# Gated mixer of two linear layers: order of the inverse, the key-query products, the roots, silu and table loads

## What is computed

```python
def chunk_gated_delta_rule(q, k, v, g, beta):
    gc = jnp.cumsum(g, axis=-1)
    seg = jnp.exp(jnp.where(incl, gc[..., :, None] - gc[..., None, :], -jnp.inf))
    kb = k * beta[..., None]
    a_mat = jnp.where(strict, jnp.einsum("nbhid,nbhjd->nbhij", kb, k) * seg, 0.0) + jnp.eye(L, dtype=f32)
    rhs = jnp.concatenate([v * beta[..., None], kb * jnp.exp(gc)[..., None]], axis=-1)
    sol = lax.linalg.triangular_solve(a_mat, rhs, left_side=True, lower=True, unit_diagonal=True)
    u, w = sol[..., :HEAD_DIM], sol[..., HEAD_DIM:]
    qk = jnp.einsum("nbhid,nbhjd->nbhij", q, k) * seg
    q_dec = q * jnp.exp(gc)[..., None]
    k_dec = k * jnp.exp(gc[..., -1:] - gc)[..., None]
```

## Time and profile before

| | us |
|---|---|
| median of 3 runs | 3536.49 (3536.39 to 3537.64) |
| profiled execution, its own time | 3531.68 |
| its span, first to last instruction | 3529.8 |
| TensorE matmul busy | 3402.0 (96% of the span) |
| VectorE busy | 1994.3 (56%) |
| ScalarE busy | 1165.2 (33%) |
| GpSimd busy | 332.8 (9%) |
| mean granted TensorE clock | 0.985 |

### The profile page before, as it was taken

The page is one execution under the profiler, slowest core; times in us unless marked ns, Lnnn a source line. Parts: engine busy times, 40 slices in busy tenths (PEclk is TensorE's granted clock), DMA queues, the critical chain, the costliest instruction groups (busy, mean ns, idle before and its releaser), DMA issues.

```text
span 3529.8 us, 49652 instructions
## 1 busy us (share of the span) xinstructions
PE 3402.0 (96%) x18508; PEld 2802.1 (79%) x18508; DVE 1994.3 (56%) x3164; ACT 1165.2 (33%) x1766; POOL 332.8 (9%) x293
## 2 busy tenths in 40 slices
PE   7999999889999999999988999999999999999999
PEld 5888877678888888887767888886778888688887
DVE  6763457667642566354766764446666625766642
ACT  4222344433221322234443322133443314343321
POOL 0000100231000000010023100111200011120002
PEclk9999999989999999999998999999999999999999
DMA  7653222104533355322210454321222332122232
GB/s 294 219 190 102 91 88 80 36 15 148 190 132 107 132 190 191 102 92 82 84 37 15 148 190 136 106 84 60 72 84 95 108 101 67 58 74 98 98 104 82
DMA packets 100835, 386.77 MB, mean 110 GB/s; under 512 B 11134, under 2 KB 12286, under 8 KB 99800
## 3 DMA queue, kind: packets, MB, share of 16 engines
q1 hardware_dynamic: 100696, 384.82, 31.8%
HBM read 382.65 MB, written 2.12 MB: 109 GB/s over the span
## 4 chain that ended last, share of the span: by engine, by line
PE 86%; DVE 7%; ACT 3%; issue 1%; DMA 1%; POOL 0%; SPq 0%; ACTq 0%; DVEq 0%; POOLq 0%
PE bank L2889 18%; PE bank L2888 18%; PE bank L2890 18%; PE bank L3014 4%; PE bank L3016 4%; PE bank L3015 4%; PE bank L2899 1%; PE bank L2901 1%; PE bank L2900 1%; PE bank L2964 1%; PE bank L2963 1%; PE bank L2962 1%; PE bank L3102 1%; PE bank L3623 1%; PE bank L3625 1%
## 5 line engine op out<-in xcount | busy, mean ns | idle before, releaser
L1119 ACT ACTIVATE wH<-wR 128x1024 fp32r<-128x1024 f32 (+2 forms) x378 | 429.2, 1135 | 1399.6 <-PE bank L2890 1305.4
L1687 DVE TENSOR_TENSOR wL<-wR,wH 128x1024 fp32r<-128x1024 f32 (+2 forms) x384 | 509.5, 1327 | 595.0 <-ACT wH L1119 590.3
L2888 PE MATMUL bank<-hH,wH 128*128 128x512 f32 x1920 | 747.7, 389 | 4.1 <-DVE wL L1687 4.1
L2889 PE MATMUL bank<-hH,wL 128*128 128x512 f32 x1920 | 747.6, 389 | 0.0
L2890 PE MATMUL bank<-hL,wH 128*128 128x512 f32 x1920 | 747.5, 389 | 0.0
L2888 PEld LDWEIGHTS bank<-hH,wH 128*128 128x128 f32 x1920 | 360.8, 188 | 79.9 <-DVE wL L1687 5.0
L2889 PEld LDWEIGHTS bank<-hH,wL 128*128 128x128 f32 x1920 | 360.7, 188 | 75.1
L2890 PEld LDWEIGHTS bank<-hL,wH 128*128 128x128 f32 x1920 | 360.8, 188 | 74.7
L2888 PE MATMUL bank<-gH,wH 128*128 128x512 f32 x924 | 359.4, 389 | 0.0
L2889 PE MATMUL bank<-gH,wL 128*128 128x512 f32 x924 | 359.4, 389 | 0.0
L2890 PE MATMUL bank<-gL,wH 128*128 128x512 f32 x924 | 359.4, 389 | 0.0
(11 more groups left out here) (496 smaller groups left out, 5247.3 us busy)
## 6 DMA issues: line engine op xcount, KB each, us to landing
wR<-in_ffn_w SPq DMA_DIRECT2D x176, 512.0 KB, 3.3
adaw<-in_ada_w SPq DMA_DIRECT2D x144, 512.0 KB, 5.2
wR<-in_ffn_w SPq DMA_DIRECT2D x64, 704.0 KB, 4.0
wR<-in_w_up SPq DMA_DIRECT2D x88, 512.0 KB, 3.3
wR<-in_w_mix SPq DMA_DIRECT2D x76, 512.0 KB, 3.3
wR<-in_w_down SPq DMA_DIRECT2D x32, 704.0 KB, 4.0
wR<-in_w_in SPq DMA_DIRECT2D x40, 512.0 KB, 3.3
wR<-in_w_out SPq DMA_DIRECT2D x16, 512.0 KB, 3.3
```

The costliest lines, as they stand in the source:

```text
L1119: act.activation(wH[n][:, 0:tiles, :], wR[n][:, 0:tiles, :], ACT.Copy).then_inc(S.w_hi, 1)
L1687: dve.tensor_tensor(wL[n][:, 0:tiles, :], wR[n][:, 0:tiles, :], wH[n][:, 0:tiles, :].bitcast(F32), ALU.subtract).then_inc(S.w_lo, 1)
L2888: pe.matmul(o, wH[n][:, k, :], rH[:, r, :], start=start and k == 0, stop=False)
L2889: pe.matmul(o, wL[n][:, k, :], rH[:, r, :], start=False, stop=False)
```

## The change

Roots: `inverse_roots` is called for keys and then for queries. ScalarE copies the keys too; it makes EGP after the 16 exponentials, then silu, the tables and the root, and after them copies the inverse. VectorE adds the bias for heads 0 and 1 first, scales head 0 only (`scaled(0)`), and scales heads 1, 2 and 3 in levels 2, 3 and 4 ahead of the low parts; the reduction for the root stands between the third and the fourth bias. It makes the key squares of a pair, begins the inverse of that pair, and leaves key-query products and, last, the decayed keys for later. GpSimd makes the first two masks before it multiplies the queries. TensorE makes the key products of pair 0, the pairs' decay rows, the key products of pair 1, the query products of pair 0, turns the inverse of heads 0 and 1, makes the query products of pair 1 and turns heads 2 and 3; before level 1 it also waits for the decayed keys. The numbers of the steps on their counters follow (not shown).

```diff
-                inverse_roots(range(4, 8))
+                inverse_roots(range(4, 6))
+                inverse_roots(range(6, 8))
...
                 for p in range(2):
-                    act.wait_ge(S.c_gp, at(S.c_gp, p + 1))
-                    act.activation(EGP[p][:, :], bank[6 + p][:, :], ACT.Exp).then_inc(S.c_a, 1)
+                    act.wait_ge(S.c_kt, at(S.c_kt, p + 1))
+                    act.activation(KTM[p][:, :, :], bank[p][:, :].rearrange("p (t c) -> p t c", t=TT),
+                                   ACT.Copy).then_inc(S.c_a, 1)
...
-                for h in range(H):
-                    act.wait_ge(S.c_xt, at(S.c_xt, h + 1))
-                    act.activation(XX[h][:, :, :], bank[h][:, :].rearrange("p (t c) -> p t c", t=TT),
-                                   ACT.Copy).then_inc(S.c_a, 1)
+                for p in range(2):
+                    act.wait_ge(S.c_gp, at(S.c_gp, p + 1))
+                    act.activation(EGP[p][:, :], bank[6 + p][:, :], ACT.Exp).then_inc(S.c_a, 1)
                 act.wait_ge(S.pm, at(S.pm, N_IN))
                 for j in range(2):
                     act.activation(pm[:, PC_Z + j, :], pm[:, PC_Z + j, :], ACT.Silu)
                 log_exp()
                 act.wait_ge(S.o_v, at(S.o_v, n_o_red(2)))
                 inverse_root(HR[:, 0:1, :], HR[:, 0:1, :], 1.0 / (2 * P), eps, S.o_rs)
+                for h in range(H):
+                    act.wait_ge(S.c_xt, at(S.c_xt, h + 1))
+                    act.activation(XX[h][:, :, :], bank[h][:, :].rearrange("p (t c) -> p t c", t=TT),
+                                   ACT.Copy).then_inc(S.c_a, 1)
...
-                dve.wait_ge(S.o_sq, at(S.o_sq, 2))
-                dve.tensor_reduce(HR[:, 0, :], YQ[:, :, :], AX.X, ALU.add).then_inc(S.o_v, 1)
...
-                for p in range(2):
-                    dve.wait_ge(S.c_kt, at(S.c_kt, p + 1))
-                    dve.tensor_copy(KTM[p][:, :, :], v4(p)).then_inc(S.c_v1, 1)
...
-                for p in range(2):
-                    for half in range(2):
-                        h = 2 * p + half
-                        f = slice(half * HD, (half + 1) * HD)
-                        dve.tensor_tensor(KB[p][:, :, f], KTM[p][:, :, f], bc(BG[:, :, h:h + 1], [P, TT, HD]),
-                                          ALU.mult).then_inc(S.c_v1, 1)
-                        dve.tensor_tensor(VB[p][:, :, f], VTM[p][:, :, f],
-                                          bc(COL[:, :, K_BE + h:K_BE + h + 1], [P, TT, HD]), ALU.mult).then_inc(S.c_v1, 1)
-                for h in range(H):
+
+                def bias_added(h):
                     dve.wait_ge(S.c_grp, at(S.c_grp, h + 1))
                     if h >= 2:
                         dve.wait_ge(S.c_a, at(S.c_a, n_c_seg(TT * (h - 1))))
                     dve.tensor_tensor(TMP[h % 2][:, :, :], v4(h), bc(causalT.unsqueeze(1), [P, TT, P]),
                                       ALU.add).then_inc(S.c_v1, 1)
+
+                def scaled(h):
+                    p, f = h // 2, slice(h % 2 * HD, (h % 2 + 1) * HD)
+                    dve.tensor_tensor(KB[p][:, :, f], KTM[p][:, :, f], bc(BG[:, :, h:h + 1], [P, TT, HD]),
+                                      ALU.mult).then_inc(S.c_v1, 1)
+                    dve.tensor_tensor(VB[p][:, :, f], VTM[p][:, :, f],
+                                      bc(COL[:, :, K_BE + h:K_BE + h + 1], [P, TT, HD]), ALU.mult).then_inc(S.c_v1, 1)
+
...
+                def key_square(h):
+                    dve.wait_ge(S.c_a, at(S.c_a, n_c_seg(TT * (h + 1))))
+                    dve.wait_ge(S.c_kk, at(S.c_kk, h + 1))
+                    dve.tensor_tensor(NN[h][:, :, :], v4(4 + h % 2), SEG[h][:, :, :], ALU.mult).then_inc(S.c_v2, 1)
+
+                def key_query(h):
+                    dve.wait_ge(S.c_kq, at(S.c_kq, h + 1))
+                    dve.tensor_tensor(QK[h][:, :, :], v4(6 + h % 2), SEG[h][:, :, :], ALU.mult).then_inc(S.c_v2, 1)
+
+                def first_inverse(h0):
+                    for h in (h0, h0 + 1):
+                        dve.wait_ge(S.c_v2, at(S.c_v2, n_c_nn(h + 1)))
+                        dve.tensor_tensor(PP[h][:, :, :], NN[h][:, :, :], bc(LM[:, 0, :].unsqueeze(1), [P, TT, P]),
+                                          ALU.mult).then_inc(S.c_v2, 1)
+                    for h in (h0, h0 + 1):
+                        dve.wait_ge(S.c_v2, at(S.c_v2, n_c_n0(h + 1)))
+                        dve.scalar_tensor_tensor(PP[h][:, :, :], PP[h][:, :, :], -1.0, bc(ident.unsqueeze(1), [P, TT, P]),
+                                                 ALU.mult, ALU.add).then_inc(S.c_v2, 1)
+                bias_added(0)
+                bias_added(1)
+                dve.wait_ge(S.sm_v, at(S.sm_v, n_bg(1)))
+                dve.wait_ge(S.c_a, at(S.c_a, n_c_ktc(2)))
+                scaled(0)
+                bias_added(2)
+                dve.wait_ge(S.o_sq, at(S.o_sq, 2))
+                dve.tensor_reduce(HR[:, 0, :], YQ[:, :, :], AX.X, ALU.add).then_inc(S.o_v, 1)
+                bias_added(3)
+                key_square(0)
+                key_square(1)
+                dve.wait_ge(S.mixc_in0, at(S.mixc_in0, 16))
+                first_inverse(0)
+                key_square(2)
+                key_square(3)
+                key_query(0)
+                key_query(1)
+                first_inverse(2)
+                key_query(2)
+                key_query(3)
                 for h in range(H):
...
-                    dve.wait_ge(S.c_a, at(S.c_a, n_c_seg(TT * (h + 1))))
                     dve.tensor_tensor(KD[p][:, :, f], KTM[p][:, :, f], bc(SEG[h][:, :, P - 1:P], [P, TT, HD]),
                                       ALU.mult).then_inc(S.c_v2, 1)
-                    dve.wait_ge(S.c_kk, at(S.c_kk, h + 1))
-                    dve.tensor_tensor(NN[h][:, :, :], v4(4 + h % 2), SEG[h][:, :, :], ALU.mult).then_inc(S.c_v2, 1)
-                    dve.wait_ge(S.c_kq, at(S.c_kq, h + 1))
-                    dve.tensor_tensor(QK[h][:, :, :], v4(6 + h % 2), SEG[h][:, :, :], ALU.mult).then_inc(S.c_v2, 1)
-                dve.wait_ge(S.mixc_in0, at(S.mixc_in0, 16))
-
-                for h in range(H):
-                    dve.wait_ge(S.c_v2, at(S.c_v2, n_c_nn(h + 1)))
-                    dve.tensor_tensor(PP[h][:, :, :], NN[h][:, :, :], bc(LM[:, 0, :].unsqueeze(1), [P, TT, P]),
-                                      ALU.mult).then_inc(S.c_v2, 1)
-                    dve.wait_ge(S.c_v2, at(S.c_v2, n_c_n0(h + 1)))
-                    dve.scalar_tensor_tensor(PP[h][:, :, :], PP[h][:, :, :], -1.0, bc(ident.unsqueeze(1), [P, TT, P]),
-                                             ALU.mult, ALU.add).then_inc(S.c_v2, 1)
...
                     elif k == 2:
+                        scaled(1)
                         early_low(4)
                     elif k == 3:
+                        scaled(2)
                         early_low(0)
                     elif k == 4:
+                        scaled(3)
                         early_low(2)
...
+                def level(k, heads=range(H)):
+                    for h in heads:
+                        u = 4 * k + h - 4
+                        if u >= 2:
+                            pool.wait_ge(S.c_z, at(S.c_z, u - 1))
+                        pool.tensor_tensor(NK[h % 2][:, :, :], NN[h][:, :, :],
+                                           bc(LM[:, k:k + 1, :], [P, TT, P]), ALU.mult).then_inc(S.c_nk, 1)
+                pool.wait_ge(S.c_a, at(S.c_a, n_c_seg(TT * H)))
+                for h in range(2):
+                    pool.wait_ge(S.c_v2, at(S.c_v2, n_c_nn(h + 1)))
+                    level(1, (h,))
                 pool.wait_ge(S.c_a, at(S.c_a, n_c_egp(2)))
                 pool.wait_ge(S.c_kq, at(S.c_kq, H))
                 for p in range(2):
                     y = pm[:, PC_Q + p, :]
                     pool.tensor_tensor(y, y, EGP[p][:, :], ALU.mult).then_inc(S.c_qd, 1)
                 pool.memset(SSt[:, :, :, :], 0.0).then_inc(S.c_qd, 1)
-
-                def level(k):
-                    for h in range(H):
-                        u = 4 * k + h - 4
-                        if u >= 2:
-                            pool.wait_ge(S.c_z, at(S.c_z, u - 1))
-                        pool.tensor_tensor(NK[h % 2][:, :, :], NN[h][:, :, :],
-                                           bc(LM[:, k:k + 1, :], [P, TT, P]), ALU.mult).then_inc(S.c_nk, 1)
-                pool.wait_ge(S.c_a, at(S.c_a, n_c_seg(TT * H)))
                 pool.wait_ge(S.c_v2, at(S.c_v2, n_c_nn(H)))
-                for k in range(1, 7):
+                level(1, (2, 3))
+                for k in range(2, 7):
                     level(k)
...
+                pe.wait_ge(S.c_a, at(S.c_a, n_c_ktc(2)))
+                for h in range(H):
+                    pe.matmul(bank[h][:, :], bc(ident[:, R_AL + h:R_AL + h + 1], [P, P]), pm[:, PS, :], start=True,
+                              stop=True).then_inc(S.c_grp, 1)
+
+                def with_keys(p, b, r, sem):
```

(39 more changed lines are left out.)

34 lines of the change are left out of this document (18 added, 16 removed).

## The result

The changed kernel takes 3540.24 us (median of 20 runs, 3534.97 to 3546.11); the kernel before, beside it on the same chip, 3535.28 (20 runs, 3531.53 to 3539.14). The ratio is 1.0013, with a 95% interval of 1.0007 to 1.0019. The forecast was 5.4 us less, and it came out some 5 us more. That is under the 0.2% that I called "same", but of the wrong sign. The profiled execution took 3534.97 (span 3533.0), 3.3 more than that of before. It was the fastest of its 20 runs, 5.3 under their median; that of before lies 3.6 under the median beside it.

What follows compares the result with a forecast made beforehand. The stage was taken as a chain of waits paced by VectorE, in a kernel mostly of dense TensorE matmuls. 2 x (-9.9 + 7.2) = -5.4 us gave 3531.1 us, range 3522 to 3539, chance 0.58.

Steps and rivals of the forecast that it cites:

- Term one: Head, up to level 1's first square: reordered keys, bias, inverse and tables save 9.9 us a layer (bounds 8.5 to 12.2).
- its two products with queries fall on the second inverse or on the decayed keys; I take 1.9: Head: GpSimd's query products delay VectorE by 0.2 to 2.3 us, taken as 1.9.
- Term two: Levels 2 to 4: scalings taking turns with GpSimd's masks cost 2.4 us a level, +7.2 a layer (bounds 2.0 to 8.5).
- the scalings slip through before them; worked through one level that is +1.8: Levels 2 to 4: late TensorE makes GpSimd's masks start later, so a level costs +1.8 us instead of +2.8.
- the slow rival: Levels 3 to 5: TensorE pauses bring half clock, which binds the levels; +3.6 us a layer, 3543.7 us; chance 0.12.
- level 5's tail and the start of the scan: Behind level 5: half clock adds 1.5 us, counted within the rival of 3543.7 us.
- Scalings are nearly free: Levels 2 to 4: ports don't change hands or GpSimd comes late; scalings cost 2.0 us a layer, 3520.7 us; chance 0.22.
- The head gives little: Head: VectorE's queue binds, GpSimd takes back over half the gain; -5.0 + 7.2 is +2.2 us a layer, 3540.9; chance 0.08.
- The clock makes it slower: Levels 3 to 5: TensorE pausing over 4 us falls to half clock and binds; +3.6 us a layer, 3543.7; chance 0.12.

Runs made afterwards that it cites:

- the scalings in level 1's wait: Changed kernel with the scalings of heads 1 to 3 moved from levels 2 to 4 to where VectorE waits for a root in level 1: 3519.72 us.
- the tables alone: Kernel before, with only silu, both table loads and the root moved ahead of the copies of the inverse: 3532.49 us, ratio 0.9987.
- with and without the reduction: With: changed kernel, scalings moved into level 1's root wait, plus one unread single-input VectorE reduction in each of levels 2 to 4: 3515.84 us; without: 3519.72 us.
- the scalings in the gap: Changed kernel with the scalings of heads 1 to 3 directly behind VectorE's YA multiplication, ahead of level 1: 3521.83 us, ratio 0.9953.
- the scalings alone: Kernel before, with only its scalings of heads 1 to 3 put into levels 2, 3 and 4: 3560.41 us, ratio 1.0069.
- the best version: Changed kernel, scalings behind YA multiplication, GpSimd's query products and state clearing behind level 1's masks, eight unread products in level 6: 3501.73 us.
- TensorE kept busy in the levels: Changed kernel with seven unread 128x256 products in TensorE's pause in each of levels 3 to 5: 3531.75 us, ratio 0.9987.

## Why the prediction was wrong

The sign was lost in two places: the turns in levels 2 to 4 were averaged down to 2.4 us a level and cost 3.1 on average, and the half clock behind level 5, which cost 2.8 and 2.6 us a layer, stood at nothing in the sum. The head gave more than forecast and didn't make up for it.

**Term one was right in its working and 1.9 us too small.** Gate rows came 2.93 us earlier (forecast 2.8), the last gate exponential ended 4.07 earlier (4.1), the first key square began 4.17 earlier (4.3), the first inverse paid 2.16 to the masks (2.2), the tables were hidden. Level 1 came 11.8 and 11.5 us earlier, not 9.9. The step that failed is "its two products with queries fall on the second inverse or on the decayed keys; I take 1.9": it cost VectorE nothing in the trace of after. It is a price that either side may pay. The run with the scalings in level 1's wait, with the same instructions in its head, has the second query product at 1.51 us in layer 1 and 1.44 in layer 2, and level 1 starts 1.1 and 1.3 us later. So here the surplus over the forecast was in part luck.

**Term two was too small, and it is where the sign went.** Levels 2 to 4 cost 2.8, 3.1 and 2.4 us in layer 1 and 2.8, 4.1 and 3.1 in layer 2, 18.4 in all where 14.4 were forecast. The turns are as I worked them out, +2.8 a level (measured with the clock held: 10.55 against 7.73). The step that failed is the average with "the scalings slip through before them; worked through one level that is +1.8". GpSimd's masks did start late, but at most the first of the two scalings slipped through (0.42, in three of the six levels); the second took 1.48 to 1.50 every time. At best that bought 0.4 us (level 4 of layer 1: 10.15 from level to level). Where TensorE came to a level at half clock, its groups of 1.1 us stood in front of VectorE's 0.6 and lengthened it (level 3 of layer 2: 11.82). The late TensorE that I counted as a relief is in sum a loss: 18.4 us for the six levels, where six times 2.8 are 16.9.

**The half clock behind level 5 was left out of the sum.** I put it into the range as luck of either sign, at nothing in the sum. In the trace it cost 2.8 and 2.6 us a layer between level 5 and the mixer's end. In layer 1 it begins 8 us ahead of the scan's first product (752 and 760.38) instead of 1 (758.9 and 759.86) and lasts 20 us instead of 10. This was the slow rival's "level 5's tail and the start of the scan", which I priced at 1.5 and then counted only there. The other two runs with scalings in their levels and nothing unread show it too: their layers take 2.3 to 3.1 us more than before from level 5 to the mixer's end. But the pauses are not all of it. Five runs without such pauses in their levels (the tables alone, the scalings in level 1's wait, with and without the reduction, and the scalings in the gap, with and without the query products behind the masks) stand at 0.3 to 1.6 us. In before the half clock ended 9.3 and 9.0 us behind the scan's first product, earlier than in any other trace without unread products in level 6, so every shift of it seen here cost something. The sum had it at nothing without a reason.

Together, for the two mixers: -23.3 from the head (forecast -19.8), +18.4 from levels 2 to 4 (+14.4), +0.2 from level 1, +5.3 from behind level 5 (0), which is +0.6 against -5.4. The medians lie 5 us apart and the mixers of these two traces 0.6. A trace is one draw of many. Between runs of nearly the same code the changed kernel's mixer varies by 2 to 3 us a layer (in layer 2 it stands at +1.75 here and at -1.53 with the query products behind the masks), and in layer 2 of the run with unread products in level 6 a decayed key did wait 1.48 us for GpSimd, with the same instructions in the head. Which part of the remaining 4 us is what stays open.

**The rivals.** "Scalings are nearly free" is refuted by the run of the scalings alone (+23 us). "The head gives little" is refuted by the trace, where the head gave 11.8 and 11.5 us; that its 3540.9 is the number nearest to the measured 3540.24 is luck. "The clock makes it slower" is half right: it wasn't bound by TensorE in every level (clock 0.75 to 0.91 in the windows from 720 to 750, VectorE 9.4 to 10.0 busy), but holding the clock in levels 3 to 5 gives 9 us, which is more than the whole difference to before. Its argument that the clock falls "in exactly such pauses at 700 and at 758.9" holds for the first place only: ahead of 758.9 TensorE's longest pause since level 4 was 1.16 us.

## What to carry to other kernels

Small operations that are moved into "an engine's spare time" have to be priced by their operands, not their length: beside a stream of GpSimd's masks one with two SBUF inputs cost a turn of GpSimd, 1.4 us each, and the one operation with a single such input that was tried cost nothing. Ask of every pause that a move makes on TensorE what runs right behind it; here the dearest products of the stage did, and eight unread products in pauses of under a microsecond bought 5.5 to 5.8 us a layer in the best version and 3.8 to 4.1 in the kernel before, but the one layer where they began at half clock ended later. And a part of a change is worth undoing singly: without the scalings in its levels the same change is 0.5% faster instead of 0.1% slower.

## What the runs showed of the hardware

Who gets the ports is not settled by the order of the program. A run of VectorE's operations 0.34 us apart kept GpSimd out for its whole length in the changed kernel (the second query product took 3.66 us in layer 1 and 3.70 in layer 2) and in layer 1 of its version with unread products in level 6 (3.66). It did not in layer 2 of that version (1.44, and a decayed key took 1.48), nor in the three runs with the scalings in level 1's wait, with TensorE kept busy in the levels, and with the scalings in the gap (1.51 in layer 1). In layer 1 the product began 0.02 or 0.03 us behind the first decayed key in all five of these runs. In levels 2 to 4, where VectorE had waited itself, the turns alternated. The page SBUF — State Buffer of the Trainium skill, section "Who interferes with whom", has whoever starts first keep the ports for its instruction; the traces agree for one instruction, and show that between back-to-back ones both outcomes occur. What decides it stays open.

The granted clock fell from 1.00 to 0.50 at 758.88 after pauses of only 0.26, 0.97 and 0.18 us in a stretch of small products (level 6 of the kernel before); the pause of 0.51 us that the expectations count among them ends at 759.86, behind the fall. With unread products in the pauses of 0.97 and 0.51 us, and pauses of 0.27 and 0.18 us left as they were, it stayed at 1.00 in both layers. Filled late, at half clock already, the same products cost time (1.65 for 0.94 us).
